# FFN 2 input of a decoder trunk on one core: seven half-size products of sums in place of eight, from the third iteration on

## What is computed

```
D_MODEL = 1024; SEQ = 512; D_FF = 2816
def swiglu(h, w_in, w_down):
    gate, up = jnp.split(h @ w_in, 2, axis=-1)
    return (jax.nn.silu(gate) * up) @ w_down
...
h = modulate(rms_norm(x, norm_gains[l, 2]), mod[:, 2, 0], mod[:, 2, 1])
x = x + 0.5 * mod[:, 2, 2][:, None, :] * swiglu(h, ffn2_w_in[l], ffn2_w_down[l])
```

## Time and profile before

| | us |
|---|---|
| median of 3 runs | 1260.99 (1260.57 to 1262.89) |
| the profiled execution | 1262.44 |
| its span, first to last instruction | 1260.7 |
| TensorE busy | 1232.3 |
| FFN 2 input, iterations 1 to 10 | 900.62 to 1124.62 |

### The profile page before, as it was taken

How to read it: one execution, slowest core, us unless ns; L and a number is a source line. 1 busy time by engine, 2 the same in 40 slices (tenths; PEclk the granted TensorE clock), 3 DMA queues, 4 the chain that set the end, 5 groups by cost and what they waited for, 6 DMA issues and landing times.

```text
span 1260.7 us, 15440 instructions
## 1 busy us (share of the span) xinstructions
PE 1232.3 (98%) x6281; PEld 1022.9 (81%) x6281; DVE 588.5 (47%) x712; ACT 415.5 (33%) x456; POOL 69.9 (6%) x110
## 2 busy tenths in 40 slices
PE   6999999999999999999999999999999999999997
...
GB/s 354 148 188 160 186 200 154 179 200 158 151 182 144 34 85 53 34 67 67 50 52 68 71 130 100 100 134 68 67 100 100 68 98 100 100 91 65 109 69 67
DMA packets 122288, 143.45 MB, mean 114 GB/s; under 512 B 4084, under 2 KB 102784, under 8 KB 122240
## 3 DMA queue, kind: packets, MB, share of 16 engines
...
q10 hardware_dynamic: 208, 0.08, 0.0%
...
## 4 chain that ended last, share of the span: by engine, by line
PE 90%; DVE 4%; ACT 3%; issue 1%; DMA 0%; ACTq 0%; DVEq 0%
PE PS L509 27%; PE PS L511 26%; PE PS L510 26%; PE PS L783 4%; PE PS L823 1%; PE PS L552 1%; PE PS L554 1%; PE PS L553 1%; PE PS L665 1%; PE PS L810 1%; PE PS L793 1%; DVE ACC0b L1561 1%; DMA PST<-in_lb_logits_dram 0%; ACT WH L1010 0%; DVE TNH L1470 0%
## 5 line engine op out<-in xcount | busy, mean ns | idle before, releaser
L509 PE MATMUL PS<-HH,WH 128*128 128x512 f32 (+1 forms) x1064 | 418.1, 393 | 4.1 <-DVE HL L1476 2.7
L511 PE MATMUL PS<-HH,WL 128*128 128x512 f32 (+1 forms) x1064 | 407.1, 383 | 0.0
L510 PE MATMUL PS<-HL,WH 128*128 128x512 f32 (+1 forms) x1064 | 406.5, 382 | 0.0
L1430 DVE TENSOR_TENSOR WL<-RAW,WH 128x2048 fp32r<-128x2048 f32 (+2 forms) x93 | 207.7, 2234 | 363.1 <-ACT WH L1010 363.1
L1010 ACT ACTIVATE WH<-RAW 128x2048 fp32r<-128x2048 f32 (+2 forms) x93 | 173.2, 1862 | 384.3 <-PE PS L511 330.9
L509 PEld LDWEIGHTS PS<-HH,WH 128*128 128x128 f32 x1064 | 200.2, 188 | 50.7 <-issue 5.7
L511 PEld LDWEIGHTS PS<-HH,WL 128*128 128x128 f32 x1064 | 200.3, 188 | 45.5
L510 PEld LDWEIGHTS PS<-HL,WH 128*128 128x128 f32 x1064 | 200.5, 188 | 41.3 <-issue 1.1
L509 PE MATMUL PS<-UH,WH 128*128 128x512 f32 (+1 forms) x416 | 148.7, 357 | 0.1
L511 PE MATMUL PS<-UH,WL 128*128 128x512 f32 (+1 forms) x416 | 146.9, 353 | 0.0
L510 PE MATMUL PS<-UL,WH 128*128 128x512 f32 (+1 forms) x416 | 146.7, 353 | 0.0
...
## 6 DMA issues: line engine op xcount, KB each, us to landing
RAW<-in_ffn_w_in_dram SPq DMA_DIRECT2D x42, 1024.0 KB, 5.1
...
RAW<-in_w_in_mix_dram SPq DMA_DIRECT2D x22, 1024.0 KB, 5.2
RAW<-in_ffn_w_down_dram SPq DMA_DIRECT2D x16, 1024.0 KB, 6.0
...
RAW<-in_w_out_dram SPq DMA_DIRECT2D x3, 1024.0 KB, 5.2
...
```

Of the source, the lines that this page charges most:

```text
L509: mm(ps, whi, ahi, start=start, stop=False)
L510: mm(ps, whi, alo, start=False, stop=False)
L511: return mm(ps, wlo, ahi, start=False, stop=stop)
L1430: V.tensor_tensor(WL[s][:, 0:size], RAW[s][:, 0:size], WH[s][:, 0:size].bitcast(F32), ALU.subtract)\
```

## The change

From iteration 2 on, a unit's product C = A x B (A: 256 weight columns against 1024 features, B: 1024 features against 512 tokens) is cut in quarters: A in a11, a12, a21, a22 (128 columns x 512 features), B in b11 to b22 (512 features x 256 tokens), C in c11 to c22 (128 columns x 256 tokens, each in the upper 256 columns of a bank of its own; half = 0 uses banks 0 to 3, half = 1 banks 4 to 7). Winograd's form of Strassen's scheme gives C by seven such products: of sums of A's quarters (s1 to s4, from RAW, once a unit) and sums of B's quarters (t1 to t4, once). Each `product` is 4 blocks x 3 = 12 matmuls of 256 columns. The sums of products are made partly in PSUM: ScalarE copies c11's first product to c21's bank (`seed_p6`) and c22's to the tile P5 (`keep_p5`), VectorE adds P5 and c21 into c12 (`seed_p5`) and later into c22 (`close_c22`), and TensorE accumulates onto what they wrote.

- Operands are no longer double-buffered as panels: WH[1] and WL[1] hold a11, a12, s1, s2, WH[0] and WL[0] s3, s4 and a place for a22 of either half. A place is refilled for the next unit once the product that reads it has ended (`prod`).
- t1, t2, t4 lie in TH and TL, in U's place of iterations 5 and later; t3 replaces h's quarter b12 in HH and HL. All four are made after the last `half_norm`, whose results are kept in the new tile TN3 rather than in the ring (`token_sums`), and split (`token_hi`, `token_lo`). Iteration 1 (`second_pair`) uses banks 4 to 7 and is otherwise as before.
- Because TH and TL occupy part of UH, the iterations from 5 on (UF_FROM) leave silu(gate) x up as fp32 in UF, at UL's address; UH and UL of these are made after the last product. FFN 2 down waits for them per piece.

```diff
+        UF = place("UF", [P, FB, T], FB * T * 4)
+        UF_FROM = 5
+        TN3 = place("TN3", [P, DB, T], 4096)
+        TS = place("TS", [P, 4, 4, T // 2], 69632)
+        TH = place("TH", [P, 3, 4, T // 2], 2 * UF_FROM * T * 4, F32R)
+        TL = place("TL", [P, 3, 4, T // 2], 2 * UF_FROM * T * 4 + 12288, F32R)
+        SW = place("SW", [P, 4, 4 * P], 98304)
+        P5 = place("P5", [P, 2, T // 2], 94208)
...
+        ROW = slice(HT, T)
+        SEVEN_FROM = 2
+        OP = dict(a11=(1, 0), a12=(1, 1), s1=(1, 2), s2=(1, 3), s3=(0, 0), s4=(0, 1), a22=((0, 2), (0, 3)))
...
+                    if piece == 1 and which == 1:
+                        pe.wait_ge(u_lo, 1 + NP + 8)
+                        pe.wait_ge(u_hi, NP + 8)
...
+            def second_pair():
+
...
+                            bank = 4 + 2 * half + m
...
+            def product(bank, op, bhi, blo, start, signal):
+
+                place_in, at_ = op
+                for k in range(4):
+                    w = slice(4 * P * at_ + P * k, 4 * P * at_ + P * (k + 1))
+                    hi, lo = WH[place_in][:, w], WL[place_in][:, w]
+                    for j, (wt, at_tokens) in enumerate(((hi, bhi), (hi, blo), (lo, bhi))):
+                        ins = mm(PS[:, bank, ROW], wt, at_tokens[:, k, :], start=start and k == 0 and j == 0,
+                                 stop=k == 3 and j == 2, skip_group_check=True)
+                ins.then_inc(signal, 1)
+
+            def seven_products(i, half):
+
+                u = seven(i, half)
+                c11, c12, c21, c22_ = (4 * half + j for j in range(4))
+                b11, b21, b22 = ((quarter_of(HH, kh, th), quarter_of(HL, kh, th)) for kh, th in ((0, 0), (1, 0), (1, 1)))
+                t1, t2, t4 = ((TH[:, j, :, :], TL[:, j, :, :]) for j in range(3))
+                t3 = quarter_of(HH, 0, 1), quarter_of(HL, 0, 1)
+                if half == 0:
+                    pe.wait_ge(silu_done, 1 + NP + i)
+                else:
+                    pe.wait_ge(umul_done, 1 + NP + i)
+                pe.wait_ge(op_lo, 3 * u + 2)
+                product(c11, OP["a11"], *b11, True, prod)
+                product(c22_, OP["s1"], *t1, True, prod)
+                pe.wait_ge(seed_b, u + 1)
+                product(c21, OP["s2"], *t2, False, prod)
+                product(c11, OP["a12"], *b21, False, prod)
+                pe.wait_ge(op_lo, 3 * u + 3)
+                pe.wait_ge(seed_c, u + 1)
+                product(c21, OP["s3"], *t3, False, prod)
+                product(c12, OP["s4"], *b22, False, prod)
+                pe.wait_ge(unit_lo, unit_of(i, half) + 1)
+                pe.wait_ge(c22, u + 1)
+                product(c21, OP["a22"][half], *t4, False, unit_done)
+
             first_units(N_F2IN, ((0, 1), (2, 3)), 2)
-            swiglu_in(N_F2IN, 1, False, first=1)
-            pe.wait_ge(u_lo, 2 * NP)
-            pe.wait_ge(u_hi, 2 * NP - 1)
+            second_pair()
+            pe.wait_ge(tok_lo, 4)
+            with pe.Fori(SEVEN_FROM, NP) as i:
+                for half in range(2):
+                    seven_products(i, half)
+            pe.wait_ge(u_lo, 1 + NP + UF_FROM)
+            pe.wait_ge(u_hi, NP + UF_FROM)
             pe.wait_ge(silu_done, 1 + 2 * NP)
 
...
-                A(HH[:, b, half_t(th)], TNH[:, j % 4, :], ACT.Identity, bias=MOD[:, 3 * DB * g + b:3 * DB * g + b + 1])\
+                normed = TNH[:, j % 4, :] if g == 1 else TN3[:, b, half_t(th)]
+                A(HH[:, b, half_t(th)], normed, ACT.Identity, bias=MOD[:, 3 * DB * g + b:3 * DB * g + b + 1])\
...
-            swiglu_in(N_F2IN, 1)
...
+            def token_hi(j):
+
+                act.wait_ge(t_made, (1, 5, 9, 13)[j])
+                if j == 1:
+                    act.wait_ge(unit_done, unit_of(1, 1) + 1)
+                A(quarter_of(HH, 0, 1) if j == 1 else TH[:, (0, None, 1, 2)[j], :, :], TS[:, j, :, :], ACT.Copy)\
+                    .then_inc(tok_hi, 1)
...
+            def sums_hi(u, j, freed):
+                act.wait_ge(s_made, 4 * u + 3 + j)
+                act.wait_ge(*freed)
+                A(WH[1 - j][:, 8 * P * (1 - j):8 * P * (2 - j)], SW[:, 2 * j:2 * j + 2, :].rearrange("p s c -> p (s c)"),
+                  ACT.Copy).then_inc(op_hi, 1)
...
+            def columns_hi(n, raw_val, freed):
...
+                A(WH[1][:, 0:8 * P].rearrange("p (k c) -> p k c", c=P), low_columns(n), ACT.Copy).then_inc(op_hi, 1)
...
+            def seed_p6(i, half):
+                u = seven(i, half)
+                act.wait_ge(prod, 6 * u + 1)
+                A(PS[:, 4 * half + 2, ROW], PS[:, 4 * half, ROW], ACT.Copy).then_inc(seed_b, 1)
+
+            def keep_p5(i, half):
+                u = seven(i, half)
+                act.wait_ge(prod, 6 * u + 2)
+                A(P5[:, half, :], PS[:, 4 * half + 3, ROW], ACT.Copy).then_inc(p5_out, 1)
...
+            def seven_ahead(i, half):
+
+                u, nxt = seven(i, half), (i, 1) if half == 0 else (i + 1, 0)
+                due = raw_due(*nxt)
+                n = N_F2IN + nxt[1]
+                last_quarter_hi(n, due, nxt[1], (unit_done, unit_of(i, half) - 1))
+                sums_hi(u + 1, 0, (prod, 6 * u + 3))
+                columns_hi(n, due, (prod, 6 * u + 4))
+                sums_hi(u + 1, 1, (prod, 6 * u + 6))
+
+            act.wait_ge(unit_done, unit_of(0, 0) + 1)
+            act.wait_ge(u_lo, 1 + NP)
+            A(SG[:, :, :], PS[:, 0:2, :], ACT.Silu).then_inc(silu_done, 1)
+            split_hi(unit_of(1, 0), raw_value(unit_of(1, 0)), unit_of(0, 0) + 1)
+            token_hi(0)
+            split_hi(unit_of(1, 1), raw_value(unit_of(1, 1)), unit_of(0, 1) + 1)
+            u_high(0)
+            token_hi(2)
+            token_hi(3)
+            silu(1, PS[:, 4:6, :], True)
+            first7 = unit_of(SEVEN_FROM, 0)
+            sums_hi(0, 0, (unit_done, unit_of(1, 0) + 1))
+            columns_hi(first7, raw_value(first7), (unit_done, unit_of(1, 0) + 1))
+            token_hi(1)
+            seed_p6(2, 0)
+            keep_p5(2, 0)
+            sums_hi(0, 1, (unit_done, unit_of(1, 1) + 1))
+            last_quarter_hi(first7, raw_value(first7), 0, (unit_done, unit_of(1, 1) + 1))
+            u_high(1)
+            seven_ahead(2, 0)
+
+            def gate_and_up(i, split, ahead=True):
+                seed_p6(i, 0)
+                keep_p5(i, 0)
+                if split:
+                    u_high(i - 1)
+                seven_ahead(i, 0)
+                up_part(i, split, ahead)
...
+            def up_part(i, split, ahead=True):
+                seed_p6(i, 1)
+                keep_p5(i, 1)
+                silu(i, PS[:, 0:4, ROW], split)
+                if ahead:
+                    seven_ahead(i, 1)
+
+            up_part(2, True)
+            with act.Fori(3, UF_FROM + 1) as i:
+                gate_and_up(i, True)
+            with act.Fori(UF_FROM + 1, NP - 1) as i:
+                gate_and_up(i, False)
+            gate_and_up(NP - 1, False, ahead=False)
...
+            act.wait_ge(prod, 6 * last7 + 3)
+            A(WH[slot(n)][:, UNIT // 2:UNIT], RAW[slot(n)][:, UNIT // 2:UNIT], ACT.Copy).then_inc(op_hi, 1)
...
+            split_hi(n + 1, raw_value(n + 1), n)
+            for i in range(UF_FROM, NP):
+                act.wait_ge(umul_done, 1 + NP + i + 1)
+                A(UH[:, 2 * i:2 * i + 2, :], UF[:, 2 * i:2 * i + 2, :], ACT.Copy).then_inc(u_hi, 1)
...
-                if j >= 4:
+                if g == 1 and j >= 4:
...
+            sh3 = MOD[:, 6 * DB:7 * DB]
+            V.tensor_tensor(SHD[:, :], sh3[:, 4:8], sh3[:, 0:4], ALU.subtract).then_inc(shift_diff, 1)
             last_blocks(2, 1, 19, N_F2IN + 1)
-            with dve.Fori(0, NP) as i:
-                swiglu_step(N_F2IN, 1, i, False, False)
+
+            def token_sums():
+
+                dve.wait_ge(t_ready, 5 * DB)
+                dve.wait_ge(shift_diff, 1)
+                n11, n12, n21, n22 = (quarter_of(TN3, kh, th) for kh, th in ((0, 0), (0, 1), (1, 0), (1, 1)))
+                V.tensor_tensor(TS[:, 0, :, :], n12, n11, ALU.subtract).then_inc(t_made, 1)
+                for k in range(4):
+                    V.scalar_tensor_tensor(TS[:, 1, k, :], n22[:, k, :], SHD[:, k:k + 1], n12[:, k, :], ALU.add, ALU.subtract)\
...
+                for k in range(4):
...
+                                           ALU.subtract).then_inc(t_made, 1)
+
...
+            def weight_sums(n, u, raw_val, after=True):
...
+                if after:
+                    dve.wait_ge(op_lo, 3 * u - 2)
+                V.tensor_tensor(s1, a21, a22, ALU.add).then_inc(s_made, 1)
+                if after:
+                    dve.wait_ge(op_lo, 3 * u)
+                V.tensor_tensor(s3, a11, a21, ALU.subtract).then_inc(s_made, 1)
+                dve.wait_ge(s_made, 4 * u + 1)
+                V.tensor_tensor(s2, s1, a11, ALU.subtract).then_inc(s_made, 1)
+                dve.wait_ge(s_made, 4 * u + 3)
```

(77 more changed lines are left out.)

110 lines of the change are left out of this document (108 added, 2 removed).

## The result

| | before | after |
|---|---|---|
| median, us | 1261.94 (1260.57 to 1266.18) | 1242.74 (1239.38 to 1245.16) |
| the profiled execution, its span | 1262.44, 1260.7 | 1239.38, 1237.6 |
| FFN 2 input, first matmul of iteration 1 to first of down (the stage) | 224.00 | 207.66 |
| of the span, the rest | 1036.7 | 1029.9 |

The ratio is 0.984 with a 95% interval of 0.9807 to 0.9874: 15.9 to 24.4 us faster. The last row of the table is the surprise: 6.8 us went where the change does next to nothing. It is one execution of each kernel, and the one after is the fastest of its four, 3.4 us under their median; by the medians the gain is 19.2 us, 4.7 more than forecast.

A forecast was written before the change was run, and what follows sets the result against it. TensorE, busy 98% of the span, was taken as the bound. Matmuls removed save 20.16 us, stalls in the way in cost 5.7, leaving 14.5: median 1260.99 to 1246.5 us, range 1244.2 to 1253.5.

The forecast's parts named there:

- SHD, one small operation, hides before a wait for TensorE.: Start of the seven-product stage: the change's extra small operation was to cost nothing.
- Removed: FFN 2 input, 18 later units: 84 narrower matmuls replace 48, 10.08 for 11.20 us each, saving 20.16 us.
- Hand-offs: Steady units: helpers deliver in time, least spare 0.5 us at seed_p5; stall 0, at most 0.5 us a unit.
- The way in: Start of the seven-product units: three TensorE stalls, together 5.7 us, between 3.5 and 8.
- (b): After iteration 1: TensorE waits for the token operand replacing HH's quarter before any product; stall 2.7 us.
- (c): Unit (2,0): ScalarE splits s3, s4 behind keep_p5, so seed_p5 is late for product 5; stall 1.3 us.
- (d): Unit (2,0): the next unit's four sums follow seed_p5, making close_c22 late for product 7; stall 1.7 us.
- The way out: FFN 2 down's start: late UH and UL work hides behind the first down units; cost 0.
- The clock falls in the stall: Rival, chance 0.27: TensorE's clock drops after the 2.6 us idle, costing 1.7 to 3.4 us; 1248.0 to 1250.
- VectorE becomes the bound: Rival, chance 0.12 including late hand-offs: slower sums and PSUM adds delay seed_p5 in half = 0 units; 1255 or 1258.
- Code is fetched anew: Rival, chance 0.06: each of 8 loop jumps waits 2.3 us for TensorE's code; 18.4 us, time 1264.9.
- the two rules: Loop jumps: a target outside a 2-page window forces a fetch; TensorE's instruction memory holds 2048, so the loop stays inside.

The follow-up runs named there:

- b_pad32: The kernel before with one unused 16-byte tile added, moving the arena's tiles up 32 bytes: ratio to the kernel before 0.9972 (0.9958 to 0.9985).
- a_pad224: The changed kernel with seven unused 16-byte tiles, its tiles 256 bytes above those of the kernel before: ratio to that kernel 0.9896 (0.988 to 0.9912).

## Why the prediction was right, and where it failed

**The failed step is "SHD, one small operation, hides before a wait for TensorE."** I priced the operation, at nothing, and not its tile. The tile moves all of the arena by 32 bytes, and the distance of matmuls changed with it throughout the program: 0.2333 to 0.2324 us at 512 columns, and in the seven products 0.1200 to 0.1187 at 256. Its worth, from runs: 0.0028 x 1263 = 3.5 us for the kernel before (b_pad32; interval 1.9 to 5.3); in the changed one the 1512 matmuls that replace 864 gain 1512 x 0.0013 - 864 x 0.0009 = 1.2 us more. 14.5 + 3.5 + 1.2 = 19.2; measured by the medians 19.2, and 18.7 when both were run again. The cause is shown in both directions, by b_pad32 and by a_pad224. That the sum meets the first number exactly is luck, with intervals of 2 to 4 us on either side. Why an address changes the distance stays open.

**Removed.** 18 x (48 x 0.2333 - 84 x 0.1200) = 20.16: right at the spacing that it took from before; a_pad224 shows 0.1200 over 1440 matmuls. With 0.2324 and 0.1187 it is 18 x (11.16 - 9.97) = 21.3.

**Hand-offs.** No steady unit waits. Groups by form after, 940 to 1102 us (before: the earlier trace rows):

```profile
L2161 DVE TENSOR_TENSOR WL<-SW,WH 128x1024 fp32r<-128x1024 f32 x31 | 38.0, 1225 | 15.9 <-ACT WH L1493 15.9
L2149 DVE TENSOR_TENSOR SW<-RAW 128x512 f32<-128x512 f32 x15 | 10.3, 684 | 0.0
L2186 DVE TENSOR_TENSOR PS<-P,PS 128x256 f32<-128x256 f32 x17 | 7.3, 429 | 5.7 <-PE PS L971 5.7
L2180 DVE TENSOR_TENSOR PS<-P,PS 128x256 f32<-128x256 f32 x16 | 6.8, 425 | 7.2 <-PE PS L971 7.2
L1515 ACT ACTIVATE P<-PS 128x256 f32<-128x256 f32 x16 | 6.2, 385 | 16.9 <-PE PS L971 16.9
L1510 ACT ACTIVATE PS<-PS 128x256 f32<-128x256 f32 x16 | 5.9, 368 | 28.5 <-PE PS L971 28.5
```

The sums, which read 128 of every 256 columns, take 0.684 us, the price of a plain 512-element operation (taken: 0.69). The PSUM writes, the cost with no row before, came in under their estimates: 0.43 us on VectorE (taken 0.48), 0.37 on ScalarE (taken 0.48). The Trainium skill ("Perfetto Trace Analysis", Optimizing Scalar/DVE Operations) gives ScalarE a lower access overhead on PSUM than on SBUF; the two rows, which both read PSUM, agree in direction: 0.368 us when it writes PSUM and 0.385 when it writes SBUF. DVE timeline of a half = 0 window after, the last two of the four sums and `seed_p5`:

```profile
1005.72 0.69 DVE L2154 TENSOR_TENSOR SW<-SW,RAW 128x512 f32<-128x512 f32 x1
1006.44 0.69 DVE L2156 TENSOR_TENSOR SW<-RAW,SW 128x512 f32<-128x512 f32 x1
1007.05 0.42 DVE L2180 TENSOR_TENSOR PS<-P,PS 128x256 f32<-128x256 f32 x1
```

`seed_p5` starts without idle, directly behind the sums, as walked; the spare that this leaves was 0.5 by the walk and 0.4 by the two runs with added sums.

**The way in.** Forecast 2.7, 1.3, 1.7, together 5.7. Measured from start to start by the runs: 3.2 for (b), 2.7 for (c) and (d), together 5.9 (the idle times alone are 2.90, 0.87 and 1.40). (a), 13 more operations for the token sums, was hidden. (c) is smaller than walked; a faster PSUM copy and add ahead of it (0.38 and 0.42 us for 0.48 each) explain part of that. The mechanism was right; that the sum came within 0.2 us is partly luck, one term being 0.5 too small and two together 0.3 too large.

**The way out.** No gap before either down unit: 0, as forecast.

**Rivals.** *The clock falls in the stall* (0.27): it did in 3 of 9 profiles, for 1.2 to 1.4 us rather than 1.7 to 3.4. Its chance was fair as far as nine profiles tell, its price too high: its lower end took the work to slow down in proportion to the clock, but at the 1.2 GHz level matmuls of 256 columns followed each other by 0.213 us (928.91 to 931.68 in a_pad224, 13 of them) and not by twice 0.120, and the gap that followed shrank in two of the three (0.63 and 0.71 for 0.87 us). *VectorE becomes the bound*: no, but 0.4 us away. *Code is fetched anew*: no. DMA queues after, 925 to 1100 us (packets, MB, share; before: the earlier trace rows):

```profile
q1 hardware_dynamic: 18720, 18.88, 33.2%
q8 instruction: 1, 0.02, 0.0%
q14 instruction: 1, 0.01, 0.0%
```

Two code packets, 0.03 MB, in a stretch with eight jumps, where before there were none: not one a jump. The Trainium skill ("Runtime: NRT & Kernel Launch", Instruction fetch mechanics) has the two rules weighed in the prediction, and refills in blocks of 256 instructions. The loop is 168 matmuls and 168 loads, 336 instructions in all, so it may lie within two such blocks; this run agrees with both rules and doesn't tell them apart. *The way in costs less*: no. None of the rivals was what happened in the kernel after itself, and the range, built from them, had no term for what moved every matmul at once.
